# State weights spread over the input stage, value and gate projections behind the tile loop, S5 weight scale on ScalarE

## The chip, the cores and the metric

The kernel runs as one program on 8 cores of one Trainium2 chip (two dies of four cores). Each core works on one half of the sequence of one of four batch entries and exchanges nothing with the others. The metric is device time in microseconds (us) of the slowest core. Engines are called PE (TensorE, matmul), ACT (ScalarE), DVE (VectorE), POOL (GpSimd) and SP (SyncE, which here only issues DMAs).

## The reference, cut to what matters

```python
z = _rms_norm(h, norm_mix_g)                     # h: 16 meta tokens, then 4096 positions, 1024 wide
p = z @ w_in                                     # 1024 -> [512 value | 512 gate | 512 S5 input]
conv_out = silu(layer_norm(conv31(value * sigmoid(gate))))
bu = einsum(b_bar, ssm_input)                    # 32 groups x 16 channels -> 64 complex states, 2 directions
states = associative_scan(lam_bar, bu)           # forward and reverse
y = einsum(c, states).real + d * ssm_input
ssm_out = gelu(y) * sigmoid(gelu(y) @ glu_w + glu_b)
h = h + concat(conv_out, ssm_out) @ w_out
h = h + relu(_rms_norm(h) @ w_ff1) ** 2 @ w_ff2
return _rms_norm(h)[:, 16:]
```

## The kernel before, in words

The program is written out by hand for each engine: `op` issues an instruction at once with the waits that its operands need, so the order of the Python code is the order of every engine's queue. `recorded` collects instructions instead, to be issued later.

**Input stage (tile loop, n = 0 to 32).** Tile 0 holds 32 special rows, tiles 1 to 16 the "far" half of the sequence (128 rows each), tiles 17 to 32 the core's own half. For each tile: `load` brings 128 x 1024 values of x into one of the buffers XT (SP's queue), `norm_sq` squares and sums them on ACT (L349), `norm_pow` takes the power -1/2 on POOL (L353, L354), `norm_z` scales on ACT (L358) into bf16, `trans` transposes in eight 128x128 pieces on PE (L372) into PSUM bank 4, and ACT or DVE copies the result (L377, L379) to one of four slots of zsl. In iteration n PE transposes tile n, ACT scales tile n+1 and squares tile n+2. Four tiles make a block of 512 positions. `u_chunk` computes one fourth of the S5 input of a block (8 matmuls of 512 columns with the scaled weights winu, L442, then an ACT copy, L455), one chunk per iteration; `bounce_write` and `bounce_read` take it through DRAM to another layout (uf, uo). `vg_chunk` does a fourth of value and gate of an own block (16 matmuls with winv, L833, a sigmoid on ACT into sgt, L838, a product on DVE into usc, L847), of 16 in all.

**Work beside the tiles.** A list bg holds recorded DVE instructions, each with a cost in ns; `pump(budget)` issues from it until the budget is used up. It takes: the scale of winu (`winu_scale`, 8 instructions), the state weights in 16 batches (`wb_batch`: six DVE operations of 128x512 elements and, per direction, two copies of powers to PSUM bank 7; then `wb_rows`: 8 transposes on PE, L628, and an ACT copy, L632), the powers for the scan (`px_setup`, 35 small operations), `far_tab` and `far_reduce` (the far half's scan, on DVE). `wb_rows` of a batch runs in the iteration after its last DVE operation (the list late), ahead of that iteration's S5 chunk. `cw_pump` issues table operations (`cw_quad`, 48 of 128x1088 elements, L470) on POOL, one or two per iteration, with scratch cta and ctb. `winv_scale` scales the other 1024 columns on DVE (L1189). `v_pair("far", ...)` (L683) multiplies uf with the weights in iterations 22 to 25.

**Behind the loop.** Remaining S5 chunks, up to three vg chunks, then the chunks of tile 0, and `v_pair("own", ...)` for 16 pairs. Then the scan on DVE and POOL (`Scan`), where the vg chunks that are left are issued, ten DVE scan operations (`vpump(10)`) between the sigmoid and the product of each. Behind the last, `uc_read` reads the gated input back, `strip_set` makes the convolution kernels of the state space part, and `conv_pair` (L922) convolves; `cd_gen` makes its weights on DVE in two buffers. Output projection and feed-forward follow.

These lines set where the loads and the chunks stand:

```python
XT = [sb("xt%d" % i, [128, D], F32, VV2 + 4096 * i if i < 3 else UO + 12288) for i in range(4)]
xbuf = [n % 4 if n < 17 else (n - 16) % 3 for n in range(33)]
...
if vq and n >= 22 and n % 2 == 0:
    vg_chunk(*vq.pop(0), (1, 5))
```

SG is the place of sgt and usc, UO that of uo, VV1 first that of the raw S5 weights, then of cta and ctb, then of the states.

Of the kernel before, what the change touches and what calls it, by code (L numbers as in the profile page):

```python
# [185 lines left out]
def _build():  # L186
# [406 lines left out]
    def wb_batch(d, m, q, st_):  # L593
# [10 lines left out]
        if d == 0:  # L604
            k1 = 15 - 8 * m
            ks = slice(k1, k1 - 8 if k1 >= 8 else None, -1)
        else:
            ks = slice(8 * m, 8 * m + 8)
# [939 lines left out]
```

How the kernel before makes its waits and increments, by code:

```python
    def _wait(self, eng, sem, val):  # L73
        d = self.waited[eng]
        if d.get(sem.name, -1) >= val:
            return
        d[sem.name] = val
        self.eng[eng].wait_ge(sem, val)
# [42 lines left out]
    def op(self, eng, fn, r=(), w=(), sig=True):  # L121
        deps = self._deps(r, w)
        o = _Op()
        o.eng = eng
        o.dma = False
        o.sem = None
        o.target = None
        for d in deps:
            self._wait_op(eng, d)
        ins = fn(self.eng[eng])
        self.eseq[eng] += 1
        o.seq = self.eseq[eng]
        if sig:
            self.ecnt[eng] += 1
            o.sigval = self.ecnt[eng]
            ins.then_inc(self.esem[eng], 1)
            self.esigs[eng].append((o.seq, o.sigval))
            if len(self.esigs[eng]) > 4096:
                del self.esigs[eng][:2048]
        else:
            o.sigval = None
        self._record(o, r, w)
        return o
# [1 line left out]
    def dma(self, eng, out, in_, r=(), w=(), final=False):  # L145
# [6 lines left out]
        for d in deps:  # L152
            self._wait_op(eng, d)
        o = _Op()
        o.eng = eng
        o.dma = True
        o.sem = self.dsems[i]
        self.dcum[i] += 16
        o.target = self.dcum[i]
        o.seq = None
        o.sigval = None
        self.eng[eng].dma_start(out=out, in_=in_).then_inc(o.sem, 16)
        self.dlast[i] = o
        self._record(o, r, w)
        if final:
```

## Time and profile before

| | us |
|---|---|
| median of 3 runs | 973.64 (971.81 to 993.13) |
| the profiled execution | 976.05 |
| its span (slowest core) | 975.0 |
| spans of the eight cores | 964.2 to 975.0 |
| busy over the span: PE, DVE, POOL, ACT | 799.1, 520.4, 383.9, 366.6 |

The profile is of one execution on the slowest core. In a timeline each row is start (us from the span's start), length (us), engine, line, operation, output<-inputs, shape, count; in brackets the idle time ahead of it and what ended it. PEld is the weight load, SPq the queue of SP. In a list of groups: busy time in us and mean ns of one, then idle time ahead. In a table by stretch: length, then busy time and count for PE, PEld, DVE, ACT and POOL, then PE's granted clock as a share of 2.4 GHz, the DMA engines' busy share and GB/s. Names beginning with s_ are SBUF tiles, p_pb are PSUM banks; L470 is the line of the helper `tt`, which issues every tensor-tensor operation.

### The profile page before, as it was taken

To read this page: it belongs to the slowest core of one execution; us is meant where nothing else is said; L and a number is where in the kernel's file an instruction comes from. 1 tells how busy PE (TensorE), PEld (TensorE's weight loads), DVE (VectorE), ACT (ScalarE), POOL (GpSimd) and SP (SyncE) were. 2 spreads that over 40 slices of the span, in tenths; PEclk is the share of its full clock that TensorE was granted. 3 is DMA by queue.
4 is the path that set the end of the run, shared out by engine and by line. 5 is a ranking of instruction groups with operands and counts; after the bars stand their busy time and mean duration, and the time that the engine had idled before them with its cause. 6 is when DMAs were issued, how large, how long until landed. Compare 5 with 4: busy or idle time off the path is not lost.

```text
span 975.0 us, 15702 instructions; the slowest of 8 cores (964.2 to 975.0 us)
## 1 busy us (share of the span) xinstructions
PE 799.1 (82%) x4584; PEld 392.5 (40%) x4584; DVE 520.4 (53%) x973; ACT 366.6 (38%) x595; POOL 383.9 (39%) x419
## 2 busy tenths in 40 slices
PE   0465666779772798669979999999999999999994
PEld 0233333335431355424544444444444444444441
DVE  5978754652888950825662334433443344334587
ACT  5776755443221352686661111111111111111353
POOL 4878740881778540200004332332324332332240
PEclk9979778899875899879998999999999999999997
DMA  8497553545129926669804232150606033060044
GB/s 244 147 223 204 119 108 86 116 76 89 27 43 109 107 33 107 143 169 239 227 3 45 42 43 45 13 75 1 87 1 82 5 34 54 3 84 1 1 173 173
DMA packets 71811, 87.27 MB, mean 90 GB/s; under 512 B 7568, under 2 KB 55824, under 8 KB 71728
## 3 DMA queue, kind: packets, MB, share of 16 engines
q1 hardware_dynamic: 56752, 66.44, 29.8%
q0 software_dynamic: 14400, 19.76, 14.7%
q8 instruction: 39, 0.64, 0.3%
q14 instruction: 44, 0.36, 0.2%
q10 hardware_dynamic: 576, 0.07, 0.0%
HBM read 86.56 MB, written 19.45 MB: 109 GB/s over the span
## 4 chain that ended last, share of the span: by engine, by line
PE 67%; DVE 14%; issue 8%; DMA 5%; ACT 3%; SPq 3%; DVEq 1%; POOL 0%; ACTq 0%; POOLq 0%
PE p_pb L1134 23%; PE p_pb L1149 23%; PE p_pb L1081 6%; PE p_pb L833 4%; PE p_pb L442 4%; SPq L162 3%; DVE p_pb L470 3%; DMA s_xt<-xl 2%; PE p_pb L1004 2%; DVE s_vo L470 2%; DVE s_cd L470 1%; PE p_pb L922 1%; PE p_pb L683 1%; PE p_pb L933 1%; PE p_pb L935 1%
## 5 line engine op out<-in xcount | busy, mean ns | idle before, releaser
L470 DVE TENSOR_TENSOR s_h<-s_h,p_pb 128x512 f32<-128x512 f32 x288 | 197.3, 686 | 260.5 <-PE p_pb L1149 254.7
L470 POOL TENSOR_TENSOR s_hid<-s_rl 128x512 bf16<-128x512 f32 x128 | 136.8, 1071 | 325.4 <-ACT s_rl L1137 304.4
L1149 PE MATMUL p_pb<-s_w2c,s_hid 128*128 128x512 bf16 x1024 | 229.9, 383 | 3.9 <-DVE s_h L470 3.9
L1134 PE MATMUL p_pb<-s_zf,s_w1c 128*128 128x512 bf16 x1024 | 228.2, 381 | 0.0
L1137 ACT ACTIVATE s_rl<-p_pb 128x512 f32<-128x512 f32 x128 | 76.4, 597 | 340.0 <-PE p_pb L1134 338.7
L1149 PEld LDWEIGHTS p_pb<-s_w2c,s_hid 128*128 128x128 bf16 x1024 | 100.9, 99 | 127.9 <-issue 10.9
L1134 PEld LDWEIGHTS p_pb<-s_zf,s_w1c 128*128 128x128 bf16 x1024 | 100.7, 98 | 122.1 <-issue 2.8
L833 PE MATMUL p_pb<-s_zsl,s_winv 128*128 128x512 bf16 x256 | 68.2, 430 | 17.2 <-ACT s_ust L455 11.2
L442 PE MATMUL p_pb<-s_zsl,s_winu 128*128 128x512 bf16 x256 | 71.9, 434 | 0.1
L833 PEld LDWEIGHTS p_pb<-s_zsl,s_winv 128*128 128x128 bf16 x256 | 26.7, 108 | 57.6 <-issue 37.7
L372 PE MATMUL p_pb<-s_ident,s_zt 128*128 128x128 bf16 (+1 forms) x264 | 23.1, 239 | 30.0 <-ACT s_zt L358 30.0
L922 PE MATMUL p_pb<-s_uc,s_cd 128*128 128x256 bf16 x160 | 22.7, 297 | 28.0 <-DVE s_st L470 21.1
L358 ACT ACTIVATE s_zt<-s_xt,s_ss 128x1024 bf16<-128x1024 f32 (+1 forms) x33 | 38.1, 1153 | 12.8 <-POOL s_ss L354 12.8
L1094 ACT ACTIVATE s_sq<-s_h 128x1024 bf16<-128x1024 f32 x32 | 33.8, 1057 | 22.9 <-DVE s_h L470 21.1
L470 POOL TENSOR_TENSOR s_cw<-s_cta,s_ctb 128x1088 bf16<-128x1088 f32 x16 | 39.9, 2493 | 0.9
L442 PEld LDWEIGHTS p_pb<-s_zsl,s_winu 128*128 128x128 bf16 x256 | 26.9, 110 | 31.2 <-issue 13.2
L847 DVE TENSOR_TENSOR s_usc<-p_pb,s_sgt 128x512 bf16<-128x512 f32 x16 | 11.0, 689 | 50.6 <-PE p_pb L833 50.6
L349 ACT ACTIVATE s_zt<-s_xt 128x1024 bf16<-128x1024 f32 (+1 forms) x33 | 34.6, 1049 | 8.9 <-DMA s_xt<-xl 8.9
L628 PE MATMUL p_pb<-s_ident,s_wsr 128*128 128x128 bf16 x128 | 11.8, 246 | 31.7 <-DVE s_wsr L470 15.0
L1081 PE MATMUL p_pb<-s_wout,s_mixc 128*128 128x512 bf16 x128 | 33.9, 384 | 2.4 <-DMA s_mixc<-scr_yc 1.8
L470 POOL TENSOR_TENSOR s_cta<-s_pwre,s_cmat 128x1088 f32<-128x1088 f32 x16 | 34.3, 2146 | 3.6 <-PE p_pb L372 1.7
L372 PEld LDWEIGHTS p_pb<-s_ident,s_zt 128*128 128x128 bf16 (+1 forms) x264 | 19.1, 109 | 40.1 <-issue 37.0
(162 smaller groups left out, 979.3 us busy)
## 6 DMA issues: line engine op xcount, KB each, us to landing
s_xt<-xl SPq DMA_DIRECT2D x32, 512.0 KB, 5.9
s_h<-xl SPq DMA_DIRECT2D x16, 512.0 KB, 17.3
s_w1c<-w_ff POOLq DMA_DIRECT2D x8, 1024.0 KB, 13.2
s_w2c<-w_ff POOLq DMA_DIRECT2D x8, 1024.0 KB, 13.8
out<-s_h SPq DMA_DIRECT2D x16, 512.0 KB, 2.7
s_wstv<-w_in SPq DMA_DIRECT2D x4, 1024.0 KB, 8.9
s_kf<-scr_rs SPq DMA_DIRECT2D x8, 384.0 KB, 16.7
s_wstu<-w_in SPq DMA_DIRECT2D x4, 512.0 KB, 11.5
```

What stands on the lines that cost most here:

```text
L349: op("act", lambda e: e.activation(z[:nr, :], xt[:nr, :], AF.Square, scale=1.0 / 32.0, accum_out=s4[:nr, 0:1]), r=[xk], w=[zk, sk])
L358: op("act", lambda e: e.activation(z[:nr, :], xt[:nr, :], AF.Identity, scale=s4[:nr, 1:2]), r=[xk, sk], w=[zk])
L372: op("pe", lambda e, k=k: e.transpose(pbv[:, k * 128:k * 128 + nr], z[:nr, k * 128:(k + 1) * 128], ident[:nr, :nr]), r=[zk, "ident"], w=[p ...
L442: op("pe", lambda e, k=k: e.matmul(pb[bi][:, o0:o0 + n], winu[:, k, c * 128:(c + 1) * 128], zrhs(kind, b, k), start=(k == 0), stop=(k == 7 ...
L470: op(eng, lambda e: e.tensor_tensor(o, a, b_, op=o_), r=r, w=w)
L833: op("pe", lambda e, k=k, bi=bi, half=half: e.matmul(pb[bi][:, 0:n], winv[:, k, (1 - half) * 512 + c * 128:(1 - half) * 512 + (c + 1) * 12 ...
L922: op("pe", lambda e, g=g, d=d, dg=dg: e.matmul(pb[bi][:, 256 * dg:256 * dg + 256], cdb[q % 2][:, g % 4, 8 * d:8 * d + 8, :], uc[:, g, d:d ...
L1081: op("pe", lambda e, k=k, half=half, src=src: e.matmul(pb[pi_][:, :], src[:, k % 4, t * 128:(t + 1) * 128], wout[:, k, half * 512:(half + ...
L1094: op("act", lambda e: e.activation(junk_ap, h[:, t, :], AF.Square, accum_out=s4[:, 0:1]), r=["h%d" % t], w=[jk, sk])
L1134: op("pe", lambda e, k=k, f=f: e.matmul(pb[pi_][:, :], w1c[fc % 2][:, k, f * 128:(f + 1) * 128], zf[:, k, b * 512:(b + 1) * 512], start=(k ...
L1137: op("act", lambda e: e.activation(rl[rb][:], pb[pi_][:, :], AF.Relu), r=[pbk[pi_]], w=["rl%d" % rb])
L1149: op("pe", lambda e, f=f, half=half: e.matmul(pb[pi_][:, :], hid[hb][:, f, ti * 128:(ti + 1) * 128], w2c[fc % 2][:, f, half * 512:(half + ...
```

## The change

The fourth x buffer moves from uo's place to SG and serves for all tiles, so `load(n + 4)` is issued in each iteration n; no vg chunk is issued in the tile loop any more, and up to four instead of three in the loop behind it. The scale of winu is issued on ACT in iterations 2 and 3. The weight batches are ordered so that one half (m) of a direction comes after the other, and bank 7 holds the powers of one half only (256 columns, key pb7a), with the table of the far scan beside it (pb7b). The budgets per iteration are 1500, 2900 or 3600 up to tile 25 (3600 or 4200 before) and 4800 from 26 on; the powers for the scan are pushed at n = 17 at a cost of 350 (n = 21 and 180 before). Weight batches that are left are issued behind the loop. `cw_pump` issues 1 or 2 operations per iteration from 17 on (2 before) and goes on in iterations 21 to 24 with a third scratch pair in the slots of zsl. `pump` issues the waiting `wb_rows` first when an operation writes its buffer.

```diff
-    XT = [sb("xt%d" % i, [128, D], F32, VV2 + 4096 * i if i < 3 else UO + 12288) for i in range(4)]
+    XT = [sb("xt%d" % i, [128, D], F32, VV2 + 4096 * i if i < 3 else SG) for i in range(4)]
-    xbuf = [n % 4 if n < 17 else (n - 16) % 3 for n in range(33)]
+    xbuf = [n % 4 for n in range(33)]
...
-        pwv = pb[7][:].rearrange("p (r k u) -> p r k u", r=2, k=16)
-        if pwb[0] != d:
-            pwb[0] = d
-            op("dve", lambda e: e.tensor_copy(pwv[:, 0], pwre[:, 0:16, d::2]), r=["pwre"], w=["pb7"])
-            op("dve", lambda e: e.tensor_copy(pwv[:, 1], pwim[:, 0:16, d::2]), r=["pwim"], w=["pb7"])
...
+        pwv = pb[7][:, 0:256].rearrange("p (r k u) -> p r k u", r=2, k=8)
+        p0 = 8 * m if d == 1 else 8 * (1 - m)
+        if pwb[0] != (d, m):
+            pwb[0] = (d, m)
+            op("dve", lambda e: e.tensor_copy(pwv[:, 0], pwre[:, p0:p0 + 8, d::2]), r=["pwre"], w=["pb7a"])
+            op("dve", lambda e: e.tensor_copy(pwv[:, 1], pwim[:, p0:p0 + 8, d::2]), r=["pwim"], w=["pb7a"])
...
-    ct = [(sb("cta%d" % k, [128, 4, 17, 16], F32, (VV1, UF)[k]), sb("ctb%d" % k, [128, 4, 17, 16], F32, (VV1, UF)[k] + 4352))
-          for k in range(2)]
+    ct = [(sb("cta%d" % k, [128, 4, 17, 16], F32, (VV1, UF, ZS + 7680)[k]), sb("ctb%d" % k, [128, 4, 17, 16], F32, (VV1, UF, ZS + 7680)[k] + 4352))
+          for k in range(3)]
...
             budget -= c
+            while late and any(k == late[0][1] for k in g[3]):
+                late.pop(0)[0]()
             P.op(*g)
...
     def winu_scale():
         for k in range(8):
-            op("dve", lambda e, k=k: e.tensor_scalar(winu[:, k, :], wstu[:, k, :], pv[:, k:k + 1], None, op0=ALU.mult),
+            op("act", lambda e, k=k: e.activation(winu[:, k, :], wstu[:, k, :], AF.Identity, scale=pv[:, k:k + 1]),
...
-    push(winu_scale, 500)
+    wuq = recorded(winu_scale)[0]
...
-    wb_list = [(1, m, q) for q in range(4) for m in range(2)] + [(0, m, q) for q in range(4) for m in range(2)]
+    wb_list = [(1, m, q) for m in range(2) for q in range(4)] + [(0, m, q) for m in (1, 0) for q in range(4)]
...
-        ahead = [m for m in (n + 3, n + 4) if 4 <= m < NT and m not in loaded and (m < 17 or m <= n + 3)]
-        for m in ahead:
-            if m < 17 or m - 3 <= n:
-                loaded.add(m)
-                load(m)
+        if n + 4 < NT:
+            load(n + 4)
...
+        if n in (2, 3):
+            for g in wuq[4 * (n - 2):4 * (n - 2) + 4]:
+                P.op(*g)
...
-        if n == 21:
-            push(px_setup, 180)
+        if n == 17:
+            push(px_setup, 350)
...
-            pump(3600 if n in (7, 8, 12, 13) else 4200)
+            pump(1500 if n in (7, 8, 12, 13) else 2900 if n % 2 == 0 else 3600)
...
-            if 0 < n < 22:
-                cw_pump(2 if n < 21 else len(cq), 0)
-            if n < 25 and len(bg) < 4 and wb_list:
+            if n < 25:
+                if n in (20, 24):
+                    while cq:
+                        P.op(*cq.pop(0))
+                else:
+                    cw_pump(2 if n % 2 else 1, 0 if n < 20 else 2)
+            if n < 24 and len(bg) < 4 and wb_list:
                 do_wb(0)
...
-                cw_pump(2, 1)
-            if vq and n >= 22 and n % 2 == 0:
-                vg_chunk(*vq.pop(0), (1, 5))
+                cw_pump(2 if n % 2 else 1, 1)
...
-            pump(4200)
+            pump(3600 if n < 26 else 4800)
...
     while uq:
         u_chunk(*uq.pop(0), "act")
+        if wb_list and len(bg) < 4:
+            do_wb(1)
         pump(2500)
-        cw_pump(2, 1)
+        cw_pump(1, 1)
...
-    while bg or late or wb_list or cw_list or cq or nv < 3:
+    while bg or late or wb_list or cw_list or cq or nv < 4:
...
-        if vq and nv < 3:
+        if vq and nv < 4:
             vg_chunk(*vq.pop(0), (1, 5))
```

## Rows read from the trace of the kernel before

**Rows 1.** Busy time by stretch, with the granted clock of PE as a share.

```profile
38.00:132.00 94.00, 61.47 (x407) 33.53 (x404) 77.26 (x120) 68.91 (x94) 77.18 (x63) 0.85 0.69 167
...
166.00:212.00 46.00, 32.88 (x194) 15.03 (x192) 27.74 (x54) 24.03 (x35) 34.04 (x26) 0.89 0.56 109
```

**Rows 2.** Timeline of ACT: z6, z17, z22, z24, z27 and z32.

```profile
39.69 1.15 ACT L358 ACTIVATE s_zt<-s_xt,s_ss 128x1024 bf16<-128x1024 f32 x1
...
97.10 1.15 ACT L358 ACTIVATE s_zt<-s_xt,s_ss 128x1024 bf16<-128x1024 f32 x1 [2.10 <-POOL s_ss L354]
...
126.96 1.15 ACT L358 ACTIVATE s_zt<-s_xt,s_ss 128x1024 bf16<-128x1024 f32 x1 [0.25 <-POOL s_ss L354]
...
147.89 1.15 ACT L358 ACTIVATE s_zt<-s_xt,s_ss 128x1024 bf16<-128x1024 f32 x1
...
171.15 1.15 ACT L358 ACTIVATE s_zt<-s_xt,s_ss 128x1024 bf16<-128x1024 f32 x1
...
209.77 1.15 ACT L358 ACTIVATE s_zt<-s_xt,s_ss 128x1024 bf16<-128x1024 f32 x1
```

**Rows 3.** The chain in order of time, tiles 27 to 29: start, length, what.

```profile
180.93 0.70 DVE s_usc L847
...
182.11 4.87 DMA s_xt<-xl
```

**Rows 4.** Timeline of PE: S5 chunks at two clocks, projection chunks.

```profile
63.04 3.40 PE L442 MATMUL p_pb<-s_zsl,s_winu 128*128 128x512 bf16 x8
...
87.67 1.89 PE L442 MATMUL p_pb<-s_zsl,s_winu 128*128 128x512 bf16 x8
...
188.88 5.30 PE L833 MATMUL p_pb<-s_zsl,s_winv 128*128 128x512 bf16 x16 [3.12 <-ACT s_ust L455]
...
225.73 10.52 PE L833 MATMUL p_pb<-s_zsl,s_winv 128*128 128x512 bf16 x48 [0.93 <-ACT s_ust L455]
```

**Rows 5.** Timeline of all engines, 137 to 318 us.

```profile
137.61 1.06 PE L683 MATMUL p_pb<-s_uf,s_wb 128*64 128x128 bf16 x16 [7.02 <-DMA s_uf<-scr_uf]
...
239.87 7.95 PE L683 MATMUL p_pb<-s_uo,s_wb 128*64 128x128 bf16 x256 [0.60 <-issue]
...
248.26 0.68 DVE L1361 COPY p_pb<-s_pximx 128x512 f32<-128x512 f32 x1
...
283.19 0.69 DVE L847 TENSOR_TENSOR s_usc<-p_pb,s_sgt 128x512 bf16<-128x512 f32 x1
...
287.19 0.68 DVE L847 TENSOR_TENSOR s_usc<-p_pb,s_sgt 128x512 bf16<-128x512 f32 x1
...
312.02 5.29 PE L922 MATMUL p_pb<-s_uc,s_cd 128*128 128x256 bf16 x30 [19.50 <-DVE s_st L470]
...
317.80 3.59 DVE L470 TENSOR_TENSOR s_cd<-s_cwx,p_pb 128x640 bf16<-128x640 bf16 x4
```

**Rows 6.** Timeline of DVE: the S5 scale.

```profile
29.50 7.36 DVE L1215 TENSOR_SCALAR s_winu<-s_wstu,s_pv 128x512 bf16<-128x512 f32 x8
```

**Rows 7.** Groups between 38 and 215 us: count, busy us, mean ns, idle before.

```profile
L349 ACT ACTIVATE s_zt<-s_xt 128x1024 bf16<-128x1024 f32 x26 | 27.3, 1050 | 7.7 <-DMA s_xt<-xl 7.7
L455 ACT CAST s_ust<-p_pb 128x512 bf16<-128x512 f32 x28 | 16.2, 580 | 14.7 <-PE p_pb L442 14.7
L632 ACT COPY s_wb<-p_pb 128x1024 bf16<-128x1024 bf16 x16 | 16.0, 1002 | 6.4 <-PE p_pb L628 6.4
...
L470 DVE TENSOR_TENSOR s_wsr<-p_pb,s_wt 128x512 bf16<-128x512 f32 x32 | 21.9, 685 | 1.7
...
L470 POOL TENSOR_TENSOR s_cw<-s_cta,s_ctb 128x1088 bf16<-128x1088 f32 x15 | 37.4, 2494 | 0.7
L470 POOL TENSOR_TENSOR s_cta<-s_pwre,s_cmat 128x1088 f32<-128x1088 f32 x14 | 30.0, 2146 | 3.2 <-PE p_pb L372 1.7
```

**Rows 8.** Groups on DVE between 123 and 150 us, powers of the state.

```profile
L470 DVE TENSOR_TENSOR s_ptx<-s_pq_re,s_pq_im 128x64 f32<-128x64 f32 x1 | 2.5, 2517 | 0.0
...
L470 DVE TENSOR_TENSOR s_pq_re<-s_ptx,s_ptx 128x64 f32<-128x64 f32 x1 | 0.2, 224 | 0.1
```

More of the change, by code:

```diff
@@ L598, in wb_batch @@
         ws, wk = wsr[st_][j], "wsr%d%d" % (st_, j)
-        pwv = pb[7][:].rearrange("p (r k u) -> p r k u", r=2, k=16)
-        if pwb[0] != d:
-            pwb[0] = d
-            op("dve", lambda e: e.tensor_copy(pwv[:, 0], pwre[:, 0:16, d::2]), r=["pwre"], w=["pb7"])
-            op("dve", lambda e: e.tensor_copy(pwv[:, 1], pwim[:, 0:16, d::2]), r=["pwim"], w=["pb7"])
[L604 to L608, printed above, removed]
+        pwv = pb[7][:, 0:256].rearrange("p (r k u) -> p r k u", r=2, k=8)
[4 more added lines that the diff above has]
+            op("dve", lambda e: e.tensor_copy(pwv[:, 1], pwim[:, p0:p0 + 8, d::2]), r=["pwim"], w=["pb7a"])
+        ks = slice(None, None, -1) if d == 0 else slice(0, 8)
         pre = pwv[:, 0, ks, 4 * q:4 * q + 4].unsqueeze(3).to_broadcast([128, 8, 4, 16])
@@ L613, in wb_batch @@
         for r in range(2):
-            tt("dve", t1[r], pre, bb[r], ALU.mult, ["pb7", "bbar"], [pbk[2 + r]])
+            tt("dve", t1[r], pre, bb[r], ALU.mult, ["pb7a", "bbar"], [pbk[2 + r]])
         for r in range(2):
-            tt("dve", wt2[st_][r][:], pim, bb[1 - r], ALU.mult, ["pb7", "bbar"], ["wt%d%d" % (st_, r)])
+            tt("dve", wt2[st_][r][:], pim, bb[1 - r], ALU.mult, ["pb7a", "bbar"], ["wt%d%d" % (st_, r)])
         for r in range(2):
@@ L619, in wb_batch @@
                [pbk[2 + r], "wt%d%d" % (st_, r)], [wk])
-        return lambda: wb_rows(d, m, q, ws, wk)
+        return (lambda: wb_rows(d, m, q, ws, wk)), wk
     def wb_rows(d, m, q, ws, wk):
@@ L685, in v_pair @@
                             start=first, stop=last, skip_group_check=True, tile_position=(0, 64 * gi)),
-                           r=["wb%d_%d_%d" % (d, m, pp // 4)] + (ufk if kind == "far" else uok), w=[pbk[bi]],
+                           r=["wb%d_%d_%d" % (d, m, pp // 4)] + (ufk if kind == "far" else uok), w=[pbk[bi]] + (["pb7a", "pb7b"] if bi == 7 else []),
                            sig=last and gi == 1)
@@ L704, in _build @@
     mask_ps = pb[5][:, 256:272]
-    fr_ps = pb[7][:, 0:48].rearrange("p (j u) -> p j u", j=3)
-    fi_ps = pb[7][:, 48:144].rearrange("p (j u r) -> p j u r", j=3, r=2)
+    fr_ps = pb[7][:, 256:304].rearrange("p (j u) -> p j u", j=3)
+    fi_ps = pb[7][:, 304:400].rearrange("p (j u r) -> p j u r", j=3, r=2)
     def far_tab():
         for k, j in enumerate((0, 7, 8)):
-            op("dve", lambda e, k=k, j=j: e.tensor_copy(fr_ps[:, k], pxre[:, j, 1::2]), r=["pxre"], w=["pb7"])
-            op("dve", lambda e, k=k, j=j: e.tensor_copy(fi_ps[:, k], pximx[:, j, 1::2, :]), r=["pximx"], w=["pb7"])
+            op("dve", lambda e, k=k, j=j: e.tensor_copy(fr_ps[:, k], pxre[:, j, 1::2]), r=["pxre"], w=["pb7b"])
+            op("dve", lambda e, k=k, j=j: e.tensor_copy(fi_ps[:, k], pximx[:, j, 1::2, :]), r=["pximx"], w=["pb7b"])
     def tab_far(jpow):
         k = (0, 7, 8).index(jpow)
-        return fr_ps[:, k], fi_ps[:, k], "pb7", "pb7"
+        return fr_ps[:, k], fi_ps[:, k], "pb7b", "pb7b"
     def hstep(eng, x1, x2, dst, src, swp, jpow, nu, nb, rk, wk, tk, tab):
@@ L1267, in _build @@
         while late:
-            late.pop(0)()
+            late.pop(0)[0]()
         if uq:
@@ L1304, in _build @@
                 if nv == 8:
-                    assert not wb_list
                     push(far_tab, 100)
@@ L1321, in _build @@
         u_chunk(*uq.pop(0), "act")
+        if wb_list and len(bg) < 4:
+            do_wb(1)
         pump(2500)
-        cw_pump(2, 1)
+        cw_pump(1, 1)
         tick()
     nv = 0
-    while bg or late or wb_list or cw_list or cq or nv < 3:
+    while bg or late or wb_list or cw_list or cq or nv < 4:
         while late:
-            late.pop(0)()
+            late.pop(0)[0]()
         if wb_list and len(bg) < 4:
             do_wb(1)
-        if vq and nv < 3:
+        if vq and nv < 4:
             vg_chunk(*vq.pop(0), (1, 5))
```

## The prediction

> **What bounds the kernel now.** I read the profile in this order: busy time by stretch, then the starts of one instruction that occurs once per tile, then the chain that ended last, then groups of instructions for the cost of one. From 513 us on (the feed-forward part) nothing is touched, so only the first 345 us count. In the tile loop no engine is full: between 166 and 212 us PE is busy 32.9 of 46 us, POOL 34.0, DVE 27.7, ACT 24.0 [rows 1]. It is a loop of waits. ACT's z instruction (L358) starts once per tile; z_n is that of tile n, issued in iteration n-1 [rows 2]. From z6 to z22 there are 16 tiles in 87.3 us, 5.45 each; z22 to z24 takes 20.9 us for two; z24 to z27 23.3 us for three; z27 to z32 38.6 us for five, 7.7 each.
>
> Why the last ones are slow is in the chain [rows 3]. Two tiles take 13.3 us: the gate product on DVE (180.93), its write on SP's queue, and behind that, in the same queue, the load of the next x tile (182.11, lands after 4.87), the square and the S5 copy on ACT behind that load (1.05, 0.19 and 0.58), then a value and gate chunk on PE from 188.88 for 5.30 us [rows 4], and the next gate product. With three x buffers a tile's load is issued only one tile ahead of its square. So six chunks in the loop cost more than their PE time.
>
> Behind the loop PE first works through the queued S5 chunks and three chunks of value and gate projection, and the own v pairs start at 239.87 [rows 5]. Then DVE's scan is the chain, to 317.8 and beyond, and PE does seven more chunks in its gaps.
>
> **The change, part by part.** (1) **S5 scale on ACT.** It removes eight DVE instructions, 7.36 us from 29.50 [rows 6], and adds eight ACT instructions of half the size of a z (1.15 us [rows 2]), so 0.58 each, 4.6 us in iterations 2 and 3. DVE could not start before its power table was done at 29.5; ACT can start at about 26.2 and has the weights ready at about 33.8, where DVE had them at 36.9. ACT then still has a copy, a z and a square in line before z6. I take z6 at 38.5 where it was 39.7: 1.2 us gained; bounds 0 and 3.
>
> (2) **State weights spread, tiles 5 to 21.** I counted, from the budgets and the costs in the diff, what each iteration issues. Before: 15 of 16 weight batches by iteration 20, one of six DVE operations for nearly every tile, 4.1 us by 6 x 0.69 [rows 7], plus a copy every other tile and the winv scales. After: 8 batches by iteration 15, the ninth by 17, then 35 small power operations in iterations 17 to 20 and batches 10 and 11 at 22 and 23; batch 12 comes at 32 and **four (13 to 16) come behind the loop**. DVE's share per tile falls from some 5 us to about 3.7 (eight batches over twelve tiles, 2.7, and the same 1.0 beside them), and the waits of PE for its weights and of DVE's copy behind them go. What is late next: POOL issues 1.5 table operations of 2.15 to 2.49 us per tile, 3.4 us, and two of the norm, 0.85 together with their gap of 0.15 each side, 4.4 us; up to tile 16 that order is not changed, and after it the 2 per tile become 1.5. ACT has z 1.15, square 1.05 and 0.19, S5 copy 0.58, half a z copy (of the size of the weight copy, 1.0) and 0.7 of a weight copy of 1.0: 4.1 [rows 7]. PE has 3.0 us when a chunk of 8 takes 1.89, and 5.2 us when it takes 3.40 [rows 4], with a transpose group of 8 at an estimated 0.6 and 1.0 in step with that and 0.75 of another for the weights. So a tile lies between 4.4 and 5.2 us; both clock levels occur in this stretch, and I take the middle, 4.8. 16 x 4.8 = 76.8 instead of 87.3: 10.5 us gained; bounds 4 and 17.
>
> What the earlier power operations cost beside POOL: of the two 128x64 operations in [rows 8] one took 2.52 us and the other 0.22, since the first began while POOL was in a table operation. Seven such POOL operations lie in iterations 17 to 20. The Trainium skill, page SBUF — State Buffer, section on the two separate sides, says that GpSimd and a VectorE operation with two SBUF inputs take one port pair in turns, each for a whole instruction; 2.52 beside 0.22 agrees. By that rule DVE could lose 7 x 2 us on top of 35 x 0.22, 22 us in four tiles, 5.5 per tile and 2.8 us more than I sum. I leave it to the range, as DVE's backlog is not what the next tile waits for there, except for its copies in tiles 18 and 20.
>
> (3) **Projections out of the loop, fourth buffer.** Six chunks leave. At tile 22 PE still waits for the far part of the scratch read until 137.61 [rows 5], which nothing shortens; behind it the first chunk, 5.9 us, is gone: 20.9 becomes 15.5. z24 to z27: a tile with two far v pairs is 0.6 + 0.6 + 1.9 on PE and 2.6 to 3 for the pairs (0.7 to 1.06 each, and a copy of 0.6 with its waits between them), 6.0: 18 instead of 23.3. z27 to z32: the chain of rows 3 is gone. The load is now issued four tiles ahead and its square comes two iterations later, about 9 us for a transfer of 5 to 7: nothing is left of that wait. Next is DVE, which now issues eight reduction operations per iteration, of the size of those in rows 7, 0.69 and 0.08 to the next (two tiles of 8 x 0.77 + 0.35 = 6.5), then POOL and ACT at 4.7 for three: 27 instead of 38.6. Together 5.4 + 5.3 + 11.6 = 22.3 gained; bounds 16 and 27. The third scratch pair for the tables lies in the slots of two z blocks; it is written by iterations 21 to 24 and the z copy of tile 25 waits for it, 2 us at most, as POOL has one operation to do in iteration 24.
>
> So z32 starts at 209.8 - 34.0 = 175.8.
>
> (4) **Behind the loop, what comes back.** Before, 30.1 us pass from z32 to the own v pairs. After, DVE has batch 12 (3.8 us), then in the four S5 iterations 16 operations, and in the next ones 4 and 6. Those last are strung on one chain, because each iteration puts the transposes of the previous batch ahead of its own projection chunk on PE, and the batch behind the gate product on DVE: transposes 1.0, chunk, product 0.9 with its wait, four or six operations (2.7 or 4.1). A chunk takes 3.5 us (a third of 10.52, [rows 4]) without a pause ahead of it and 5.3 after one (188.88, a pause of 3.12); here three of four have a pause of 3 to 5 us ahead. Counted from z32: weights of batch 14 ready at 15.3; first chunk done at 21.6, batch 15 at 25.2, second chunk at 31.6, batch 16 at 36.3, third at 42.7, fourth at 46.2, then the four special chunks, 3.5: 49.7; with full clock throughout 43. I take 49: **18.9 us lost**; bounds 12 and 24.
>
> (5) **Twelve chunks instead of seven in the scan stage.** Ten DVE operations stand ahead of each product. Before, the seventh product ended at 287.87, 39.6 us after the stage's first DVE instruction (248.26) [rows 5]. Five more follow at a little under the pitch of the last two, 283.19 to 287.19: 3.7 us, as ten small operations take DVE 3.0 and the product 0.69, and a chunk takes PE 3.5. So the last product ends 58.1 us after the stage began. DVE's own work grows by only 5 x 0.69 = 3.5 us. But the reads of the gated input are issued behind the last product, and the first convolution came at 312.02, 24.1 us behind it. DVE's third set of convolution weights (317.80) overwrites what convolutions 0 and 1 read, so it can't start until they are done, 3.7 us (two thirds of the 5.29 of three, and a wait), 27.8 us behind the last product: 58.1 + 27.8 = 85.9 us after the stage began where it was 69.5: **16.4 us lost**. DVE came there 29.9 us after the last product; 50 small operations of that, some 14.5, now lie ahead of it, so it gets there after 15.4 and stands still for 12. Bounds 10 and 20. From there the order is as before, shifted.
>
> **Sum:** -1.2 - 10.5 - 22.3 + 18.9 + 16.4 = +1.3 us. The profiled execution took 976.05 us, of which 975.0 is the span; the median of the three runs is 973.64, 2.4 lower. I put the sum on the median: 975.
>
> **Rivals.** *The tail stays short and the loop reaches POOL's floor.* 43 us behind z32 and 4.4 per tile: 6 + 6.4 less, 962.5. For it speaks that 48 matmuls in a row took 0.22 each there [rows 4]; against it that the chunk after a pause in rows 4 took 5.3. *The chunks of part 5 are hidden.* Then only DVE's 3.5 us stand: 975 - 12.9 = 962. For it: seven chunks of 3.5 fill 24.5 of 40 us there, so PE has room. Against: the read of the gated input ends last for the first convolution, and it stands behind all products. *PE's clock sets the loop* (the slower side). With value and gate chunks gone PE has less to do, and if it is granted 1.2 GHz through tiles 5 to 31 its 5.2 to 5.5 us is above all others; the mean granted clock was 0.85 to 0.89 with more work in it [rows 1]. It decides from 4.8 us per tile on; 0.6 x 21 tiles + 4 in the tail = 16.6: 991.6. *The spreading does nothing*, if 5.45 per tile was from waits other than DVE's weights: 10.5 back, 985.5. The change of part 3 can't fail to remove the chain, since its first link, the product, is no longer in the loop.
>
> **How the numbers follow.** Forecast 975: 0.55, its own range 966 to 984. Short tail 0.13; hidden chunks 0.11; both 0.04 (949); PE's clock 0.11; spreading void 0.06. The range 961 to 988 leaves out the double gain and most of the slow clock. Two per cent is 19.5 us, about what a measurement of this kernel can tell from no change: faster 0.06 (both gains, or one with the loop's bound), slower 0.06, the same 0.88.
>
> **What would show it.** Right: z32 at 170 to 182; no product on DVE before z32; the own v pairs some 49 us behind z32, with PE waiting for DVE's weights and chunks at 5.3 us; twelve chunks in the scan stage; the first convolution 24 us behind the last product; DVE idle some 12 us ahead of the third set of weights; the rest of the kernel unchanged in length. Wrong: tiles 5 to 21 still at 5.4 us, a tail of under 40 us, or a stage behind it that grows by 4 us alone.

## The result and the profile after

The changed kernel takes 987.65 us (median of 5 runs, 986.79 to 1010.72), the kernel before 973.64 (5 runs beside them, 971.58 to 1080.99). The ratio is 1.015, 95% interval 1.0131 to 1.017: 14 us more, where 1.3 more had been forecast. In some executions of either kernel the cores of one die or of both are granted a lower clock and take longer (the times above 990 us here), and the ratios leave these out. The profiled execution took 987.65, its span 986.6 on core 1; spans of the eight cores:

```profile
core 0: 977.6 us, clock 0.922
core 1: 986.6 us, clock 0.919
...
core 6: 983.6 us, clock 0.925
core 7: 977.2 us, clock 0.922
```

Which core is slowest changes from one execution to the next, so I read the same marks in the timeline of each of the eight cores and took their mean. z_n is again the start of ACT's z for tile n, "pairs" the first own v pair, "stage" the first DVE instruction of the scan stage, "third" the third set of convolution weights; us:

| | z6 | z22 | z24 | z27 | z32 | pairs | stage | last product ends | first conv | third | span |
|---|---|---|---|---|---|---|---|---|---|---|---|
| before | 39.8 | 126.0 | 145.1 | 169.1 | 206.4 | 236.5 | 245.3 | 284.9 | 308.6 | 314.8 | 971.2 |
| after | 38.9 | 119.2 | 133.2 | 153.6 | 182.2 | 231.8 | 241.1 | 299.5 | 323.5 | 327.9 | 980.0 |

The last tile is 24.2 us earlier, the third set of weights 13.1 us later. Two parts give the loop's gain back: from z32 to the own pairs 49.6 us instead of 30.1, and from the stage's start to the third set 86.8 instead of 69.5.

The same views as before, of core 1. Busy time by stretch (columns as in rows 1):

```profile
38.00:132.00 94.00, 56.64 (x368) 29.75 (x368) 72.31 (x105) 65.54 (x92) 78.93 (x66) 0.85 0.78 185
166.00:212.00 46.00, 28.96 (x145) 13.45 (x142) 35.80 (x72) 20.14 (x29) 30.16 (x21) 0.81 0.45 78
```

Against [rows 1], PE does less in the second stretch and is granted 0.81 instead of 0.89, while DVE is busier (35.8 instead of 27.7). It is not the same work: the stretch held tiles alone before, and now holds 20 us of tiles and 26 us of what follows them. Timeline of ACT, z6, z22, z24, z27 and z32, beside [rows 2]:

```profile
39.23 1.15 ACT L358 ACTIVATE s_zt<-s_xt,s_ss 128x1024 bf16<-128x1024 f32 x1 [0.17 <-POOL s_ss L354]
...
123.72 1.15 ACT L358 ACTIVATE s_zt<-s_xt,s_ss 128x1024 bf16<-128x1024 f32 x1 [0.77 <-POOL s_ss L354]
...
137.45 1.15 ACT L358 ACTIVATE s_zt<-s_xt,s_ss 128x1024 bf16<-128x1024 f32 x1
...
157.82 1.15 ACT L358 ACTIVATE s_zt<-s_xt,s_ss 128x1024 bf16<-128x1024 f32 x1
...
186.39 1.15 ACT L358 ACTIVATE s_zt<-s_xt,s_ss 128x1024 bf16<-128x1024 f32 x1
```

Timeline of PE from there to the own pairs; before, this was one run of 48 matmuls in 10.52 us [rows 4]. L625 transposes weights, L830 is the projection:

```profile
175.04 1.01 PE L372 MATMUL p_pb<-s_ident,s_zt 128*128 128x128 bf16 x8 [7.29 <-DVE s_zsl L379]
...
202.12 1.01 PE L625 MATMUL p_pb<-s_ident,s_wsr 128*128 128x128 bf16 x8 [3.18 <-DVE s_wsr L470]
202.92 6.19 PE L830 MATMUL p_pb<-s_zsl,s_winv 128*128 128x512 bf16 x16
212.90 1.01 PE L625 MATMUL p_pb<-s_ident,s_wsr 128*128 128x128 bf16 x8 [3.78 <-DVE s_wsr L470]
213.70 5.92 PE L830 MATMUL p_pb<-s_zsl,s_winv 128*128 128x512 bf16 x16
224.53 1.01 PE L625 MATMUL p_pb<-s_ident,s_wsr 128*128 128x128 bf16 x8 [4.91 <-DVE s_wsr L470]
225.34 8.68 PE L830 MATMUL p_pb<-s_zsl,s_winv 128*128 128x512 bf16 x32
```

The other half of that loop, on DVE: gate product, then a weight batch.

```profile
219.80 0.69 DVE L844 TENSOR_TENSOR s_usc<-p_pb,s_sgt 128x512 bf16<-128x512 f32 x1 [7.16 <-PE p_pb L830]
220.41 1.29 DVE L470 TENSOR_TENSOR p_pb<-p_pb,s_bbar 128x512 f32<-128x512 f32 x2
221.60 1.28 DVE L470 TENSOR_TENSOR s_wt<-p_pb,s_bbar 128x512 f32<-128x512 f32 x2
222.80 1.48 DVE L470 TENSOR_TENSOR s_wsr<-p_pb,s_wt 128x512 bf16<-128x512 f32 x2
```

Each engine waits for the other in turn: PE 3.18, 3.78 and 4.91 us for the weights, DVE 7.16 for the chunk. Nothing overlaps, and the two chunks right behind a pause take 6.19 and 5.92 us for 16 matmuls, where the next 32 took 8.68.

The scan stage beside [rows 5]: timeline of DVE up to the last two products, of PE at the first convolution, and of DVE at the third set of weights.

```profile
246.67 0.68 DVE L1363 COPY p_pb<-s_pximx 128x512 f32<-128x512 f32 x1
...
300.55 0.69 DVE L844 TENSOR_TENSOR s_usc<-p_pb,s_sgt 128x512 bf16<-128x512 f32 x1
...
304.35 0.69 DVE L844 TENSOR_TENSOR s_usc<-p_pb,s_sgt 128x512 bf16<-128x512 f32 x1
```

```profile
329.66 5.74 PE L919 MATMUL p_pb<-s_uc,s_cd 128*128 128x256 bf16 x30 [17.48 <-DMA s_uc<-scr_uc]
```

```profile
334.20 3.60 DVE L470 TENSOR_TENSOR s_cd<-s_cwx,p_pb 128x640 bf16<-128x640 bf16 x4 [11.03 <-PE p_pb L919]
```

The last product ends 58.4 us after the stage began, the first convolution waits 17.48 us for the read of the gated input and comes 24.6 us behind that product, and DVE stands still for 11.03 us ahead of its third set of weights.

### The profile page after: what moved, and what is told of

The parts are those of the page before. It is cut to its first block, busy times and chain, and to the rows that moved or that the text cites. A ratio compares the mean times of both kernels' runs of the same rounds, so it can differ in the third digit from the quotient of the medians.

```text
span 986.6 us, 15721 instructions; the slowest of 8 cores (976.7 to 986.6 us)
## 1 busy us (share of the span) xinstructions
PE 798.3 (81%) x4584; PEld 392.3 (40%) x4584; DVE 532.9 (54%) x969; ACT 371.0 (38%) x603; POOL 383.7 (39%) x419
## 4 chain that ended last, share of the span: by engine, by line
PE 62%; DVE 14%; issue 9%; DMA 7%; ACT 5%; SPq 2%; DVEq 0%; ACTq 0%
PE p_pb L1131 22%; PE p_pb L1146 22%; PE p_pb L1078 6%; DVE p_pb L470 3%; DMA s_xt<-xl 3%; SPq L162 2%; PE p_pb L830 2%; DVE s_vo L470 2%; DMA s_wstv<-w_in 2%; DMA s_uc<-scr_uc 2%; PE p_pb L919 1%; PE p_pb L1001 1%; DVE s_yv L470 1%; ACT s_sil L972 1%; DVE s_vf L470 1%
## 5 line engine op out<-in xcount | busy, mean ns | idle before, releaser
L372 PE MATMUL p_pb<-s_ident,s_zt 128*128 128x128 bf16 (+1 forms) x264 | 25.6, 255 | 65.7 <-ACT s_zt L358 47.4
L830 PE MATMUL p_pb<-s_zsl,s_winv 128*128 128x512 bf16 x256 | 66.4, 421 | 7.5 <-DVE s_usc L844 6.6
L830 PEld LDWEIGHTS p_pb<-s_zsl,s_winv 128*128 128x128 bf16 x256 | 26.5, 107 | 45.9 <-issue 23.9
L919 PE MATMUL p_pb<-s_uc,s_cd 128*128 128x256 bf16 x160 | 23.6, 305 | 25.2 <-DMA s_uc<-scr_uc 17.5
L470 POOL TENSOR_TENSOR s_ctb<-s_pwim,s_cmat 128x1088 f32<-128x1088 f32 x16 | 34.4, 2149 | 0.0
L625 PE MATMUL p_pb<-s_ident,s_wsr 128*128 128x128 bf16 x128 | 12.3, 253 | 26.5 <-DVE s_wsr L470 19.7
## 6 DMA issues: line engine op xcount, KB each, us to landing
s_kf<-scr_rs SPq DMA_DIRECT2D x8, 384.0 KB, 16.2
```

The costliest lines, as they stand in the source:

```text
L372: op("pe", lambda e, k=k: e.transpose(pbv[:, k * 128:k * 128 + nr], z[:nr, k * 128:(k + 1) * 128], ident[:nr, :nr]), r=[zk, "ident"], w=[p ...
L470: op(eng, lambda e: e.tensor_tensor(o, a, b_, op=o_), r=r, w=w)
L830: op("pe", lambda e, k=k, bi=bi, half=half: e.matmul(pb[bi][:, 0:n], winv[:, k, (1 - half) * 512 + c * 128:(1 - half) * 512 + (c + 1) * 12 ...
L919: op("pe", lambda e, g=g, d=d, dg=dg: e.matmul(pb[bi][:, 256 * dg:256 * dg + 256], cdb[q % 2][:, g % 4, 8 * d:8 * d + 8, :], uc[:, g, d:d ...
```

## The experiments

Ratios are to the kernel before, timed on the same chip; "core mean" is the mean over the eight cores of the profiled execution.

**1. Weights as before** (on the changed kernel). All 16 batches are done by tile 23 again; the rest of the change stands.

```diff
-        if n == 17:
-            push(px_setup, 350)
+        if n == 21:
+            push(px_setup, 180)
-            pump(1500 if n in (7, 8, 12, 13) else 2900 if n % 2 == 0 else 3600)
+            pump(3600 if n in (7, 8, 12, 13) else 4200)
-            if n < 24 and len(bg) < 4 and wb_list:
+            if n < 25 and len(bg) < 4 and wb_list:
-            pump(3600 if n < 26 else 4800)
+            pump(4200)
```

> The changed kernel with the budgets, the place of the scan powers and the conditions of the kernel before, so that all 16 weight batches are issued by tile 23; the projections stay behind the loop. Theory (the tail is a serial chain of DVE's last four batches): the own v pairs stand 30 to 33 us behind the last z instead of 50, the tile loop is up to 6 us longer, and the time falls by 14 us to about 973. Rival (the tail is long because four projection chunks stand in it, whatever DVE does): the distance stays at 45 us or more and the time at 984 or above.

Measured 973.02 us, ratio 0.9971 (0.9955 to 0.9987). Timeline of PE (core 4, where z32 starts at 190.4):

```profile
202.78 3.61 PE L830 MATMUL p_pb<-s_zsl,s_winv 128*128 128x512 bf16 x16 [0.93 <-ACT s_ust L455]
206.78 10.52 PE L830 MATMUL p_pb<-s_zsl,s_winv 128*128 128x512 bf16 x48 [0.39 <-ACT s_sgt L835]
...
221.00 5.17 PE L680 MATMUL p_pb<-s_uo,s_wb 128*64 128x128 bf16 x122 [0.69 <-issue]
```

The tail is the old one, 30.1 us in core mean. Tiles 6 to 22 take 90.7 us instead of 80.3, tiles 22 to 32 57.7 instead of 63.0. So the spreading gains about 10 us in the first stretch, loses 5 in the second and 19.5 in the tail. Another part of the change loses some of that gain: up to tile 22 the kernel before takes 86.2 us in its profiled execution, and 88.2 and 88.0 in experiments 5 and 9, whose code is the same up to there. Experiments 7 and 8, with the old budgets too, take 90.4 and 90.6. So some 2.5 us are lost to something else in the change, and no run looks for it.

**2. Two chunks per iteration in the tail** (on the changed kernel): eight chunks there, one ahead of and one behind DVE's operations, so eight and not twelve are left for the scan stage.

```diff
-        if vq and nv < 4:
-            vg_chunk(*vq.pop(0), (1, 5))
-        nv += 1
-        pump(3500)
+        if nv < 4:
+            vg_chunk(*vq.pop(0), (1, 5))
+        pump(3500)
+        if nv < 4:
+            vg_chunk(*vq.pop(0), (0, 4))
+        nv += 1
```

> The changed kernel with eight instead of four value and gate chunks in the loop behind the tiles, two in each iteration, one ahead of DVE's weight operations and one behind them; eight are left for the scan stage. Theory (PE stands idle in the tail while DVE makes weights, and each chunk in the scan stage delays the last product by 3.7 us): the scan stage up to the third set of convolution weights shrinks by 15 us, the tail grows by 0 to 4, the time is about 975. Rival (the chunks cost PE time wherever they stand): the tail grows by 4 x 3.5 and the time stays at 987.

The profiled execution took 974.97 us. Only one more of the four can be compared, with 976.32 us, so there is no ratio with an interval; both lie some 12 us below the changed kernel, where the theory had 975. In core mean the tail is 53.3 us (49.6), for four chunks more, and the stage to the third set 72.1 (86.8). Timeline of PE in the tail (core 0):

```profile
203.34 9.11 PE L830 MATMUL p_pb<-s_zsl,s_winv 128*128 128x512 bf16 x31 [0.22 <-issue]
212.78 0.61 PE L625 MATMUL p_pb<-s_ident,s_wsr 128*128 128x128 bf16 x8 [0.33 <-DVE s_wsr L470]
213.22 7.07 PE L830 MATMUL p_pb<-s_zsl,s_winv 128*128 128x512 bf16 x31
```

With a second chunk between, PE waits 0.33 us for the weights instead of 3.78, and 32 matmuls take 7.07. The chunks were nearly free in the tail (3.7 us for four) and cost 3 to 4 us each in the scan stage (14.7 for four).

**3. Early reads** (on the changed kernel): the read of a block of the gated input is issued as soon as its four products are written, not behind the last product.

```diff
+    nread = 0
     while vq:
...
         tick()
+        while (nread + 1) * 4 <= 15 - len(vq):
+            uc_read(nread)
+            nread += 1
     tick()
-    for b in range(4):
+    for b in range(nread, 4):
         uc_read(b)
```

> The changed kernel with the read of the gated input of each block issued as soon as its four products are written, instead of all four behind the last product. Theory (the first convolution waits for that read, which starts behind the last product): the first convolution comes about 10 us instead of 24 behind the last product, DVE's wait of some 11 us ahead of its third set of convolution weights goes, and the time falls by 10 to 12 us to about 976. Rival (DVE's own chain sets it, or the reads are limited by how fast they go beside other work): within 3 us of the changed kernel.

Measured 975.6 us, ratio 1.0021 (1.0009 to 1.0032). Timelines of PE and of DVE (core 7, stage from 244.52, last product 302.19):

```profile
313.17 6.05 PE L919 MATMUL p_pb<-s_uc,s_cd 128*128 128x256 bf16 x30 [3.15 <-DVE p_pb L470]
```

```profile
320.92 3.59 DVE L470 TENSOR_TENSOR s_cd<-s_cwx,p_pb 128x640 bf16<-128x640 bf16 x4
```

The bracket says it: the convolution waits 3.15 us for DVE instead of 17.48 for the DMA, and DVE reaches its weights without standing still. The first convolution comes 9.9 us behind the last product instead of 24.0, the stage to the third set is 76.4 us.

**4. Scale on DVE** (on the changed kernel): only the scale of the S5 weights goes back.

```diff
-            op("act", lambda e, k=k: e.activation(winu[:, k, :], wstu[:, k, :], AF.Identity, scale=pv[:, k:k + 1]),
+            op("dve", lambda e, k=k: e.tensor_scalar(winu[:, k, :], wstu[:, k, :], pv[:, k:k + 1], None, op0=ALU.mult),
```

> The changed kernel with the S5 weight scale back on DVE, in the same iterations 2 and 3. Theory (worth about 1 us): z of tile 6 about 1 us later and the time 0 to 2 us longer. Rival (the scale on ACT delays the z of tiles 4 and 5 and costs time): 1 to 3 us shorter.

Measured 991.34 us (986.83 to 1069.49), ratio 1.0148 (1.0117 to 1.0178), that of the changed kernel itself. Timelines of DVE with this edit (core 5) and of ACT in the changed kernel (core 1):

```profile
29.23 7.71 DVE L1214 TENSOR_SCALAR s_winu<-s_wstu,s_pv 128x512 bf16<-128x512 f32 x8
```

```profile
26.68 2.54 ACT L1214 ACTIVATE s_winu<-s_wstu,s_pv 128x512 bf16<-128x512 f32 x4
...
32.11 2.54 ACT L1214 ACTIVATE s_winu<-s_wstu,s_pv 128x512 bf16<-128x512 f32 x4
```

ACT is done at 34.7 where DVE is at 36.9, but z6 starts at 39.5 with DVE and at 38.9 with ACT, and by z22 (120.6 and 119.2) that can't be told from the scatter of other runs (tiles 6 to 22 take 80.2 to 81.6 us in experiments 2, 3, 4 and 6, which have the same budgets). The move is worth nothing that the time shows.

**5. Early reads in the kernel before.** The edit of 3 on the other kernel.

> The kernel before, with the read of the gated input of each block issued as soon as its products are written. Theory (in the kernel before DVE's own scan, not this read, was last for the third set of convolution weights: it came there 29.9 us after the last product, the second convolution was done after about 27.6): the time stays within 3 us of the kernel before, though the first convolution comes earlier. Rival (the read was already last, so that the gain of early reads has nothing to do with the twelve chunks): 5 to 12 us faster than before.

Measured 974.53 us, ratio 0.9981 (0.9948 to 1.0013). Here the first convolution comes 9.8 us behind the last product instead of 23.7, yet nothing is gained. Timeline of PE (core 6):

```profile
299.64 3.81 PE L922 MATMUL p_pb<-s_uc,s_cd 128*128 128x256 bf16 x20 [4.67 <-DVE p_pb L470]
310.46 2.29 PE L922 MATMUL p_pb<-s_uc,s_cd 128*128 128x256 bf16 x10 [7.01 <-DVE p_pb L470]
```

The third convolution waits for DVE all the same. In the kernel before the read was late but hidden; five more chunks moved it onto the path.

**6. Three buffers** (on the changed kernel): the buffers and the load rule of the kernel before, projections still behind the loop.

```diff
-    xbuf = [n % 4 for n in range(33)]
+    xbuf = [n % 4 if n < 17 else (n - 16) % 3 for n in range(33)]
-        if n + 4 < NT:
-            load(n + 4)
+        for m in (n + 3, n + 4):
+            if 4 <= m < NT and m not in loaded and (m < 17 or m <= n + 3):
+                loaded.add(m)
+                load(m)
```

> The changed kernel with three x buffers from tile 17 on, and each load issued three tiles ahead, as before; the projections stay behind the loop. Theory (what made the late tiles slow was the load's place in the queue behind the gate product, and a projection chunk between): the late tiles stay within 3 us of the changed kernel's and the time at 986 to 990. Rival (the distance of the load matters by itself, as a transfer of 5 to 7 us then has one tile of about 5 us to land): z22 to z32 8 to 15 us longer and the time 995 to 1002.

Measured 985.95 us, ratio 1.0125 (1.0104 to 1.0146); z22 to z32 takes 61.9 us, against 63.0 with four buffers. So the load distance is worth nothing here. What is left to have made the late tiles slow is the load's place behind the product's write in SP's queue, and the chunk itself; no run takes these two apart.

**7. Weights and reads** (on the changed kernel): the edits of 1 and 3 together.

> The changed kernel with both edits that were tried by themselves: all weight batches in the loop with the budgets of before, and early reads of the gated input. Theory (the two losses stand in different stages and add): 973 less 10 to 12, about 962, faster than both kernels. Rival (the scan stage is then set by DVE or by the products, so that the earlier start of the stage is lost again): 969 to 973.

Measured 962.18 us, ratio 0.9872 (0.9844 to 0.99). The two losses are separate and add: tail 30.1 us, stage to third set 76.0. Waits by engine, 161 to 190 us (core 7; us in total, times, longest):

```profile
PE p_pb L372 <- DVE s_zsl L379: 9.8, 3, 4.7
```

**8. And copies on ACT** (on 7): the z copies of tiles 26, 28, 30 and 32 go from DVE, which has eight reduction operations per tile there, to ACT.

```diff
-        trans(n, "act" if n % 2 or n < 7 else "dve")
+        trans(n, "act" if n % 2 or n < 7 or n > 25 else "dve")
```

> The kernel with all weights in the loop and early reads, and besides the z copies of tiles 26, 28, 30 and 32 on ACT instead of DVE. Theory (in tiles 26 to 32 PE waits for a copy that stands behind eight reduction operations in DVE's queue): z27 to z32 3 to 6 us shorter and the time 3 to 5 us below that kernel. Rival (ACT, with 1.0 us more per second tile, becomes the bound): no difference or 1 to 2 us longer.

Measured 956.57 us (955.83 to 957.44), ratio 0.982 (0.9802 to 0.9838). The same view:

```profile
PE p_pb L372 <- ACT s_zt L358: 8.4, 4, 3.3
```

PE no longer waits for DVE's copy, and z27 to z32 takes 21.7 us instead of 26.8. This version is the fastest of all here.

**9. Projections alone** (on the kernel before): no chunk in the tile loop and four instead of three behind it; spreading, buffers and scale as before.

```diff
-            if vq and n >= 22 and n % 2 == 0:
-                vg_chunk(*vq.pop(0), (1, 5))
...
-    while bg or late or wb_list or cw_list or cq or nv < 3:
+    while bg or late or wb_list or cw_list or cq or nv < 4:
...
-        if vq and nv < 3:
+        if vq and nv < 4:
```

> The kernel before with one part of the change: no value and gate chunk in the tile loop, and up to four in the loop behind it; three x buffers, weights, budgets and S5 scale as before. Theory (this part gains 17 to 20 us in the tiles 22 to 32, costs 3.5 us in the tail for one more chunk, and gives back 17 us in the scan stage with its twelve chunks): the time stays within 4 us of the kernel before, 972 to 977, and the serial tail was all that made the changed kernel slower. Rival (the chunks behind the loop cost less than that): 962 to 968.

Measured 967.73 us, ratio 0.9936 (0.9914 to 0.9958). In core mean z22 to z32 falls from 80.4 to 58.7 us, the tail stays at 30.0, the stage to the third set is 85.6. That part alone is a gain of 6.2 us (4 to 8). That is outside the theory's range and at the upper end of the rival's. The scan stage gives back 16.1 us, as expected; it is the tail that costs nothing, where 3.5 us had been put. Before, four chunks stood behind z32 as well, since the chunk of iteration 32 comes after it: 16 matmuls at 214.28 us on core 4, then the 48 of [rows 4]. Timeline of PE, late tiles and tail (core 6):

```profile
174.23 1.01 PE L372 MATMUL p_pb<-s_ident,s_zt 128*128 128x128 bf16 x8 [4.76 <-DVE s_zsl L379]
...
201.35 10.52 PE L833 MATMUL p_pb<-s_zsl,s_winv 128*128 128x512 bf16 x47 [0.39 <-ACT s_sgt L838]
```

**10. Milder spread** (on 8): between the two budgets, with all 16 batches done in the loop.

```diff
-            pump(3600 if n in (7, 8, 12, 13) else 4200)
+            pump(2100 if n in (7, 8, 12, 13) else 3600)
...
-            pump(4200)
+            pump(4800 if n < 26 and n != 24 else 4200)
```

> The kernel with all weights in the loop, early reads and late copies on ACT, with budgets of 2100 and 3600 up to tile 16 and 4800 from 17 to 23, so that the sixteenth weight batch is still issued by tile 24. Theory (spreading pays in tiles 5 to 21 as long as no batch is left behind the loop): z22 2 to 5 us earlier and the time 1 to 4 us below that kernel's 956.6. Rival (what the loop gains from spreading goes with the four batches it did not have to make): z22 and the time within 1.5 us.

Measured 959.41 us, ratio 0.9836 (0.98 to 0.9872): no gain over 8. Both expectations had z22 wrong: it comes 9.5 us earlier (120.7), but z24 to z27 takes 24.4 us instead of 17.2. Waits by engine, 150 to 182 us (core 1):

```profile
PE p_pb L625 <- DVE s_wsr L470: 7.0, 1, 7.0
ACT s_wb L629 <- PE p_pb L625: 6.2, 1, 6.2
```

The batches that slid back stand ahead of the far pairs in PE's queue, and PE waits 7.0 us for one of them. The mean of the cores is 1.0 us shorter than in 8 (951.1 and 952.1 over all executions of each), while the slowest core lies 7.0 us above that mean instead of 3.4; this distance is taken up again below.

## Why the prediction missed by its size

The profiled executions differ by 11.6 us (987.65 and 976.05) where 1.3 was summed, and the median that the sum was put on lay 2.4 us below the profiled execution of before. The 10.3 us between 11.6 and 1.3, in core means but for the last row:

| | forecast | measured |
|---|---|---|
| start (z6) | -1.2 | -0.9 |
| tiles 6 to 22 | -10.5 | -5.9 |
| tiles 22 to 32 | -22.3 | -17.4 |
| tail | +18.9 | +19.5 |
| own pairs | 0 | +0.5 |
| scan stage to the third set | +16.4 | +17.3 |
| the rest | 0 | -4.3 |
| slowest core above the mean | 0 | +2.8 |
| sum | +1.3 | +11.6 |

**The failed step is the loop's gain**, 34.0 us forecast ("z32 starts at 209.8 - 34.0 = 175.8"), 24.2 measured. The terms that were mis-sized are the rate of tiles 6 to 22, which left waits for transfers at nothing, and tiles 24 to 32, which left out what the two parts of the change do to each other. It failed in two ways.

*The levels were too low by 6.4 us*: z32 is at 182.2 in core mean. Of these, 3.5 are in tiles 6 to 22, "the middle, 4.8" per tile where 5.0 was measured. Experiment 1 shows that the mechanism is there: with the old budgets the same code needs 90.7 us instead of 80.3. The excess is not spread evenly over the cores. Between z6 and z18 cores 0, 2, 4 and 7 take 57.4 to 59.3 us, so 4.8 to 4.9 per tile as forecast, and cores 1, 3, 5 and 6 take 61.7 to 64.8, so 5.1 to 5.4; the last is what the prediction had named as a sign of being wrong. Waits by engine, 38 to 132 us, core 1 (us in total, times, longest):

```profile
DVE s_winv L1186 <- DMA s_wstv<-w_in: 13.8, 4, 4.0
ACT s_zt L349 <- DMA s_xt<-xl: 6.7, 3, 4.8
```

Cores 3, 5 and 6 wait 11.4 to 16.2 us for the same two transfers, the four others 0.5 to 2.1 or not at all. An x load lands after 6.6 to 7.1 us (median) on the waiting cores and after 4.6 to 5.4 on the others. In the six profiled executions with a spread (the changed kernel and experiments 2, 3, 4, 6 and 10), the 22 cores that wait under 8 us in all take 56.4 to 60.1 us for these tiles, and the 26 that wait longer 60.5 to 66.2. The prediction's rate went by POOL, ACT and PE alone. In the kernel before no core's DVE waits for these weights there: it reaches them later. This is read from traces; no run changes the transfers alone, and why they are slower on some cores stays open.

From 18 to 22 it is 4.9 us per tile (z18 at 99.5 in core mean), so the power operations that the change moves ahead of tile 22 were rightly left out of the tiles' rate there. DVE was held up by them all the same. The chain that ended last runs through DVE from 106.6 to 139.1 us without another engine in between; two of its rows:

```profile
115.08 2.05 DVE s_pq_re L470
...
120.61 2.11 DVE s_pq_im L470
```

Seven DVE operations (one of them a copy) take 1.95 to 2.57 us between 108 and 128 us, like the first of [rows 8], where others of their size take 0.2 to 0.3. Each of the seven lies beside a POOL table operation, and eight operations of 128x16 elements behind them (from 128.62 us) take 6.07 us together, which took 2.12 in the kernel before. For the operations with two inputs that agrees with what the Trainium skill (SBUF — State Buffer, section on the two separate sides) says of a VectorE operation with two SBUF inputs beside GpSimd. It is paid just after tile 22, and that I had left out (no run takes these hold-ups away by themselves, so their share is not shown): DVE comes late to batches 10 and 11, whose transposes stand ahead of a chunk in PE's queue. Timeline of PE, tiles 24 and 25:

```profile
135.44 1.01 PE L372 MATMUL p_pb<-s_ident,s_zt 128*128 128x128 bf16 x8 [1.62 <-DVE s_zsl L379]
139.33 1.01 PE L625 MATMUL p_pb<-s_ident,s_wsr 128*128 128x128 bf16 x8 [2.88 <-DVE s_wsr L470]
```

z24 to z25 takes 8.8 us in core mean, against 4.8 in experiments 1 and 9, where the weights are done by then. z22 to z24 is 14.0 us where 15.5 was forecast, and z24 to z27 20.4, not 18. z27 to z32 is 28.6, not 27: the z copy on DVE behind eight reduction operations, 7.29 us of PE's wait in one tile. I had summed those operations, but not that the copy stands behind them all; experiment 8 takes the copy away and gets 5.1 us back. Taken by itself the removal of the projections was sized rightly: experiment 9 measures 21.7 us for it (22.3 forecast). What I missed is that the two parts disturb each other.

*The baseline was too high by 3.4 us.* I took before's loop from its slowest core, and z6 to z32 there is longer than the mean of the cores (170.1 against 166.6 us). The core that was slowest for one execution is no measure of the loop, but neither is the mean of one execution: in experiment 5, with the same code in the loop, it is 169.1. Measured against that, the loop is 25.8 us shorter after the change, not 23.3, where 32.8 was forecast, and the levels remain the larger miss. For the same reason two rows of the table can't be taken as effects of the change. Over 34 executions of the kernel before the mean span of its cores is 968.9 us, and the profiled one had 971.2; for the changed kernel it is 981.0 over three, and 980.0 in the profiled one. So the change costs some 12 us in core mean. The "rest" was long in that one execution of before: from the first matmul with the scan kernels (s_kf) to the end it took 602.5 us, in experiment 5, whose code is the same from there on, 599.0, and after the change 598.2. How far above the mean the slowest core lies (3.4 to 7.0 us, averaged over the executions of one kernel) is explained in part. In the changed kernel core 1 is 6.6 us above the mean at the end, and 4.1 of these arise between z6 and z18, where it waits for the transfers; in experiment 10 the cores are up to 6.8 us apart in the same tiles (56.4 and 63.2).

**What held.** The tail, link by link on core 1, counted from z32: transposes of batch 14 at 15.7 (15.3 forecast for its weights), first chunk done at 22.7 (21.6), batch 15 at 26.5 (25.2), second chunk 33.2 (31.6), batch 16 at 38.1 (36.3), last chunk 47.6 (46.2), own pairs 51.1 (49.7). The two chunks behind a pause took 0.6 and 0.9 us more than the 5.3 of [rows 4]. The scan stage, core 1 but where said: last product 58.4 us after its start (58.1), first convolution 24.0 behind it in core mean (24.1), DVE idle 11.0 (12). Experiments 1, 2 and 3 show the causes by taking each away.

**The rivals.** The short tail (43 us) and the hidden chunks fell with these numbers. PE's clock was the likeliest name for the slower side, and it is not the cause: between 38 and 132 us the granted clock is 0.85 with and without the change. It fell where PE had less to do and more to wait for: from z27 to z32 it was 0.78 (core 1) instead of 0.87 (core 4 before), but PE was busy for only 16.9 of these 28.6 us, and experiment 8 makes these tiles 5.1 us shorter by taking copies off DVE. The spreading isn't void. The slower side came by none of these; it came as a smaller gain against losses of the forecast size.

**What makes the changed kernel slower** than the one before is thus the spreading, in the form that leaves four batches behind the loop: with it 987.65, without it 973.02 us. Moving the projections gains by itself, and the reads behind the last product keep most of that gain from showing: 16 us lost where 22 are gained. With both mended the change is worth 1.3% (experiment 7), and 1.8% with the copies on ACT.

## What to carry to other kernels

Work that is moved off a loop is only free where something covers it: ask at its new place which engine pair then takes turns, and give the waiting one a second piece of independent work between (experiment 2 put four more chunks into 3.7 us). When more work is put ahead of a final read, issue the read piece by piece; a late read that costs nothing today (experiment 5) costs 12 us once more work lies ahead of it (experiment 3). And when a difference between two large sums is forecast, take both from the mean of the cores, and from more than one execution where there are any: from z6 to z32 the slowest core took 3.5 us more than the mean of its own execution and 0.9 more than that of another, where the sum was 1.3. An engine that gets its work done earlier will also ask for its data earlier: give the transfers that feed it a term of their own (DVE's wait for weights, nothing before, up to 13.8 us after).

## What I had not expected of the hardware

What PE's clock does behind a short pause. Table by stretch, granted clock third from the end: the changed kernel's three runs of chunks in the tail, and one of experiment 2.

```profile
203.00:209.00 6.00, 6.00 (x18) 2.08 (x15) 0.07 (x1) 2.89 (x3) 0.00 (x0) 0.57 0.53 46
213.80:219.60 5.80, 5.80 (x17) 1.91 (x15) 0.00 (x0) 1.61 (x2) 0.00 (x0) 0.61 0.00 0
225.40:233.80 8.40, 8.40 (x34) 3.47 (x32) 0.69 (x1) 2.49 (x5) 0.00 (x0) 0.81 0.05 19
```

```profile
213.30:220.20 6.90, 6.85 (x33) 2.95 (x31) 3.13 (x7) 2.21 (x3) 0.00 (x0) 1.00 0.12 39
```

After waits of 3.18 and 3.78 us the whole next chunk ran at 0.57 and 0.61, so for most of its length at the lower level of 1.2 GHz, 5.9 to 6.2 us for 16 matmuls; after a wait of 0.33 us twice as many took 7.07 at 1.00. PE also had more work all around it in that experiment, so the pause by itself is not singled out. Of each round of some 11 us in the tail, about 2.5 are this. And the slowest core of one and the same program changes: over the 34 executions of the kernel before each of the eight cores is the slowest in three to seven, with about 1% between the fastest and the slowest (964.2 and 975.0 us in the profiled execution of before).
